# Tokens on partitions in the last MLP's output, an earlier context half in the convolution, another order in the opening

## The chip, the cores and the metric

The kernel runs on one core of one Trainium2 chip. The metric is device time of the whole kernel in microseconds (us); the kernel before takes 3229.1 us as the median of three runs (3225.97 to 3230.03). The trace is one further execution, recorded by the hardware profiler.

## The reference

Width 1024, 256 latent tokens (`x`) and 256 context tokens, all in fp32. Only the latents come out. Cut to the parts around the change:

```python
s_lat, s_ctx = silu(c), silu(c_ctx)
mod_l, mod_c = s_lat @ ada_w[i] + ada_b[i], s_ctx @ ada_w[i] + ada_b[i]     # six chunks of 1024 each
h_lat = rms_norm(x) * (1 + mod_l[1]) + mod_l[0]                             # opening: first layer's input
...                                                     # retention + FFN, differential attention + FFN
x = x + g * (silu(a) * b) @ ffn_w_out                                       # ffn1_out, latents only
# second model, layer 0: convolution mixer, on latents and context
u = x * (1 + sc1) + sh1                                                     # uc likewise, from ctx_2
a = u @ w_pw1 + b_pw1;  a = a[:, :1024] * sigmoid(a[:, 1024:])
a = dwconv(a, w_dw)                                                         # 31 taps per channel
...                                                     # pw2, layer norm, MLP, mLSTM layer
# second model, layer 1: the last MLP
h = layer_norm(ALPHA * h + g2 * (square(relu(modulate(h) @ w1)) @ w2), ln2_g, ln2_b)   # 1024 -> 4096 -> 1024
```

## The kernel before

One program with a hand-written stream for each engine and semaphores between them. The activations lie in `X[128, 8, 512]`: features on partitions in 8 chunks, tokens on the free dimension, latents in columns 0 to 255 (`L_COLS`), context in 256 to 511 (`C_COLS`).

**Matmuls.** Each fp32 product is three matmuls (`split_mm`, L622 to L626): both operands are split into a high and a low part, and high by high, low by high and high by low are added in one PSUM bank. The weights come as one list of 512 KB tiles of 128x1024, in the order of the table `PHASES`. A tile goes from SP's DMA into `RAW` (four slots) to ACT (`hi`, L1366 in the trace), to DVE (`lo`, L1848), to PE; the weights run three tiles ahead of PE (`LOOKAHEAD`). In nearly all phases the weights are the stationary operand and 256 or 512 tokens move. In `ml_o` it is the reverse: 128 tokens are stationary and 512 weight columns move. In `bank<-a,b` of the trace, a moves and b is stationary (`w_hi,xm_hi` is `ml_o`).

**Opening** (PE from L833, ACT, DVE from L2099). The 16 first tiles of the modulation weights (`ada_first`) are read by SP in order, then weight tiles 0 to 3. POOL's queue reads vectors, `X`, identity, ones and the rope table. PE waits for those, sums the squares of `X` (16 matmuls of 512 columns at L823), then multiplies tiles 11 to 15 (L841, 16 matmuls of two columns each). DVE forms the products of tiles 0 to 10 (L1859, twice per tile) with the reciprocal of the standard deviation (L1905) after tile 7, copies PE's part from PSUM (L2106), and builds the first `h_hi`, `h_lo`.

**ffn1_out and convolution.** `ffn1_out` is latents only. Then DVE adds the residual of 8 chunks (L1937, `residual`), and `modulate(4, TOK)` builds `h_hi`, `h_lo` chunk by chunk, latent half and context half (`h_lo` at L1924). PE waits for `x_upd` 32 (the latents' last residual) and has `h_lo_done` waits in its first tile. `pw1` has 16 weight tiles; a pair of tiles makes 128 channels of both halves of the gated unit. DVE's `conv_input(p)` (L2407 and on) turns the pair into `conv_in_hi`, `conv_in_lo` (L2420); PE's `conv_taps(p)` sums the taps with diagonal matrices. PE's order (from L1061):

```python
conv_taps(0)
for t in range(LOOKAHEAD, 16):
    pw1_tile(t)
    if t % 2 == 0:
        conv_taps(t // 2 - 1)
```

**Last MLP** (`mlp(1, ...)`, L1127). `mlp1_in` gives 4096 features, squared ReLU, kept as `mlp_hi`, `mlp_lo`; ahead of it PE sums features and squares for the layer normalisation and waits for `std_done`. `mlp1_out` is `gemm_cols`: 32 weight tiles, each stationary for 8 banks of 128 features x 256 tokens, 24 matmuls a tile. Then, one after the other: residual on DVE (L1937), `feature_sums` on PE (L829), mean and centering on DVE (L2067, L2069), squares on ACT and `square_sums` on PE (L823), the square root on ACT, `norm_x` on DVE (L1905, L2490, L2493), and one DMA of 1 MB (L511).

`own(...)` lets an engine wait for its own last instruction where the next one reads its result.

## Time and profile before

| What | Value |
|---|---|
| median of three runs | 3229.1 us (3225.97 to 3230.03) |
| the profiled execution's own time | 3219.72 us |
| its span, first instruction to last | 3217.8 us |
| mean granted TensorE clock | 0.974 of full speed |
| PE busy | 3056.8 us, 95% |
| DVE busy | 2058.1 us, 64% |
| ACT busy | 1200.0 us, 37% |
| POOL busy | 194.8 us, 6% |

The execution's own time is 1.92 us longer than its span. A matmul's length in the trace runs from issue to modelled end, and successive matmuls overlap, so the distance between starts is what a stream costs.

### The profile page before, as it was taken

Reading aid. Unit: us, or ns where it says so; the run is one execution under the profiler, and the core shown is the slowest. Engines: PE = TensorE matmul, PEld = TensorE weight load, DVE = VectorE, ACT = ScalarE, POOL = GpSimd, SP = SyncE. Lnnn points to the kernel's source line nnn. Section 1 sums busy time; section 2 is a strip of 40 time slices with the busy share of each in tenths; the row PEclk is TensorE's granted clock in tenths of the full one; section 3 lists DMA queues with packets and bytes.
Section 4 is the critical chain, followed back from the end, with each engine's and each line's share of the span. In section 5 each row is a group of like instructions: output and inputs, shape, how many; then the busy total and the mean of one; then the engine's idle time right before and its main releaser. Section 6 shows DMA issues by size and latency. Waiting matters only on the chain.

```text
span 3217.8 us, 43502 instructions
## 1 busy us (share of the span) xinstructions
PE 3056.8 (95%) x15904; PEld 2538.1 (79%) x15904; DVE 2058.1 (64%) x3192; ACT 1200.0 (37%) x1788; POOL 194.8 (6%) x165
## 2 busy tenths in 40 slices
PE   6999999999999899898999999999999999998998
PEld 4778578888887699776888887798778777966897
DVE  6963578877754756687798867542188433544654
ACT  3223434332243664554341324432245322312553
POOL 1300000000021000000030300000000000001110
PEclk8999999999999999999999999999999999988999
DMA  6662054666522156310266543662356332523453
GB/s 255 203 216 92 20 183 170 209 209 236 171 84 92 53 170 222 117 54 27 79 203 213 169 167 106 221 214 98 118 177 219 127 113 92 183 101 124 145 183 125
DMA packets 124806, 479.53 MB, mean 149 GB/s; under 512 B 13705, under 2 KB 14729, under 8 KB 122209
## 3 DMA queue, kind: packets, MB, share of 16 engines
q1 hardware_dynamic: 119984, 443.08, 40.6%
q0 software_dynamic: 4656, 34.17, 2.8%
q8 instruction: 114, 1.87, 0.2%
q14 instruction: 52, 0.42, 0.0%
HBM read 459.37 MB, written 17.83 MB: 148 GB/s over the span
## 4 chain that ended last, share of the span: by engine, by line
PE 83%; DVE 9%; ACT 3%; issue 3%; DMA 1%; SPq 0%; DVEq 0%; ACTq 0%; PEldq 0%
PE bank L624 25%; PE bank L625 24%; PE bank L626 24%; PE bank L1343 2%; PE bank L878 1%; PE bank L1292 1%; ACT tmp L1366 1%; DVE ada_junk_a L1859 1%; DVE w_lo L1848 1%; DVE diff_col L2333 1%; ACT w_hi L1366 1%; PE bank L1229 1%; DMA ada_first<-in_ada 0%; PE bank L823 0%; DVE ada_first L1859 0%
## 5 line engine op out<-in xcount | busy, mean ns | idle before, releaser
L1848 DVE TENSOR_TENSOR w_lo<-w_raw,w_hi 128x1024 fp32r<-128x1024 f32 x620 | 756.4, 1229 | 700.0 <-ACT w_hi L1366 682.7
L1366 ACT ACTIVATE w_hi<-w_raw 128x1024 fp32r<-128x1024 f32 x623 | 654.3, 1055 | 963.9 <-PE bank L626 936.8
L624 PE MATMUL bank<-h_hi,w_hi 128*128 128x512 f32 (+1 forms) x2160 | 748.2, 346 | 47.3 <-DVE h_lo L1924 21.9
L625 PE MATMUL bank<-h_lo,w_hi 128*128 128x512 f32 (+1 forms) x2160 | 738.8, 342 | 0.0
L626 PE MATMUL bank<-h_hi,w_lo 128*128 128x512 f32 (+1 forms) x2160 | 738.4, 342 | 0.0
L624 PEld LDWEIGHTS bank<-h_hi,w_hi 128*128 128x128 f32 x2160 | 414.7, 192 | 103.8 <-issue 47.2
L625 PEld LDWEIGHTS bank<-h_lo,w_hi 128*128 128x128 f32 x2160 | 415.0, 192 | 46.9 <-issue 1.2
L626 PEld LDWEIGHTS bank<-h_hi,w_lo 128*128 128x128 f32 x2160 | 414.6, 192 | 45.5
L624 PE MATMUL bank<-w_hi,xm_hi 128*128 128x512 f32 x512 | 199.5, 390 | 1.7 <-DVE tmp L2606 0.9
L626 PE MATMUL bank<-w_hi,xm_lo 128*128 128x512 f32 x512 | 199.3, 389 | 0.0
L625 PE MATMUL bank<-w_lo,xm_hi 128*128 128x512 f32 x512 | 199.2, 389 | 0.0
L624 PE MATMUL bank<-mlp_hi,w_hi 128*128 128x256 f32 (+1 forms) x528 | 175.8, 333 | 0.0
L625 PE MATMUL bank<-mlp_lo,w_hi 128*128 128x256 f32 (+1 forms) x528 | 174.8, 331 | 0.0
L626 PE MATMUL bank<-mlp_hi,w_lo 128*128 128x256 f32 (+1 forms) x528 | 174.8, 331 | 0.0
L624 PE MATMUL bank<-xm_hi,w_hi 128*128 128x512 f32 (+1 forms) x512 | 173.1, 338 | 1.7 <-issue 0.8
L626 PE MATMUL bank<-xm_hi,w_lo 128*128 128x512 f32 (+1 forms) x512 | 172.8, 337 | 0.0
L625 PE MATMUL bank<-xm_lo,w_hi 128*128 128x512 f32 (+1 forms) x512 | 172.7, 337 | 0.0
L1366 ACT ACTIVATE tmp<-bank 128x512 f32<-128x512 f32 (+1 forms) x124 | 62.3, 502 | 181.9 <-PE bank L626 107.4
L566 POOL TENSOR_TENSOR mlp_lo<-tmp,mlp_hi 128x512 f32 (+1 forms) x64 | 92.5, 1445 | 608.9 <-DVE tmp L2543 559.6
L624 PE MATMUL bank<-ffn_hi,w_hi 128*128 128x256 f32 (+1 forms) x360 | 120.3, 334 | 2.8 <-issue 1.4
L625 PE MATMUL bank<-ffn_lo,w_hi 128*128 128x256 f32 (+1 forms) x360 | 119.7, 332 | 0.0
L626 PE MATMUL bank<-ffn_hi,w_lo 128*128 128x256 f32 (+1 forms) x360 | 119.7, 332 | 0.0
(404 smaller groups left out, 4952.4 us busy)
## 6 DMA issues: line engine op xcount, KB each, us to landing
w_raw<-in_weights SPq DMA_DIRECT2D x623, 512.0 KB, 3.3
ada_ring_f<-in_ada SPq DMA_DIRECT2D x56, 512.0 KB, 3.2
ada_ring_g<-in_ada SPq DMA_DIRECT2D x44, 512.0 KB, 3.3
ada_ring_b<-in_ada SPq DMA_DIRECT2D x38, 512.0 KB, 4.2
ada_ring_a<-in_ada SPq DMA_DIRECT2D x32, 512.0 KB, 3.3
ada_first<-in_ada SPq DMA_DIRECT2D x16, 512.0 KB, 16.2
v_spill<-ml_v POOLq DMA_DIRECT2D x1, 4096.0 KB, 13.3
o_spill<-ml_o_grp POOLq DMA_DIRECT2D x4, 1024.0 KB, 4.8
```

The lines of the kernel that those rows point to most:

```text
L566: pool.tensor_tensor(mlo[:, t, 0:T], tmp(s % 2, T), mhi[:, t, 0:T].bitcast(F32), SUB)\
L624: mm(out, lhs[0], rhs[0], start=start, stop=False)
L625: mm(out, lhs[0], rhs[1], start=False, stop=False)
L626: return mm(out, lhs[1], rhs[0], start=False, stop=stop)
L878: last = mm(PS[3 + t][:, :], ATT[:, a, i0:i0 + P], RV[:, v, 512 * h:512 * (h + 1)], start=n == 0, stop=n == len(keys) - 1)
L1229: last = mm(PS[0][0:16, :], gate_part(2, f - 1), tmp((f - 1) % 2), start=f == 1, stop=f == MLC)
L1292: last = mm(PS[2 * (h % 2) + j // 2][:, (j % 2) * LAT:(j % 2 + 1) * LAT], MK[:, 4 * h + d, j * P:(j + 1) * P], MQ[:, 4 * h + d, :], start= ...
L1343: last = mm(PS[6 + n % 2][:, :], MPT(h, d)[:, j, t * P:(t + 1) * P], MV2[:, j, 512 * h:512 * (h + 1)], start=i == 0, stop=i == len(keys) - 1)
L1366: return nc.scalar.activation(out, in_, func, **kw)
L1848: V.tensor_tensor(WLO[:, slot, :], RAW[:, slot, :], WHI[:, slot, :].bitcast(F32), SUB)\
L1859: ins = V.scalar_tensor_tensor(junk[:, :] if st == 0 else tile, tile, 1.0, rows[:, st, :], MUL, MUL, accum_out=MOD[:, bass.ds(a * 2 + st, 1)])
L2333: own(V.reduce_max(DCOL[:, col + 12:col + 13], PS[2 * (u % 2) + m][:, :], AX.X))
```

## The change

**Opening.** SP reads `X` between modulation tiles 5 and 6 (before, POOL's queue did), and weight tiles 0 to 2 after modulation tile 9. A semaphore stands for two modulation tiles instead of four. PE takes tiles 3, 5, 7, 9, 11, 13 and 15, three of them ahead of the square sums and four behind; DVE takes the other nine, with the reciprocal after tile 12. The rope table is loaded after POOL's three `w_lo`.

**Convolution.** DVE and ACT build the context half of `pw1`'s input during `ffn1_out` (steps 8 to 16 of its 22). After `ffn1_out` only the latent half is left, and residual, product and low part of a chunk follow each other by chunk. PE waits for `x_upd` 28 instead of 32. `pw1_tile(3)` stands ahead of `conv_taps(0)`. One feature sum moves ahead of the last taps.

**Last MLP's output.** `out_tokens` makes 128 tokens stationary and moves 512 weight columns, the left column half first (16 weight tiles of two blocks of 128 rows x 512 columns), then the right one: 12 matmuls a tile, 384 in all. Between the halves PE turns `X` with 16 transposes. The last three tiles are used for tokens 0 to 127 first, then for tokens 128 to 255. The gate becomes a row: eight diagonal matrices built by DVE during `down`, two fp32 matmuls with ones ahead of `mlp1_in`, two copies on ACT. The layer normalisation is done on DVE per 128 tokens: gate product, sum, `bn_stats`, `bn_aggr`, centering, reciprocal and output, with the square root on ACT; the sums of the left half are done during the right one. Gain and bias come as rows by one DMA of 1 MB on POOL's queue. The output leaves in four DMAs of 256 KB. The three zero tiles at the end of the weight list are gone.

The diff, cut to its core:

```diff
+CTX2_AT = 8
...
+ADA_TENSOR = (3, 5, 7, 9, 11, 13, 15)
...
 for n in range(ADA_FIRST):
-    sp.dma_start(ADA_RAW[:, n, :], ada[n]).then_inc(S(f"ada_first{n // 4}"), 16)
-for n in range(SLOTS):
-    sp.dma_start(RAW[:, n, :], weights[n]).then_inc(raw_full[n], 16)
+    sp.dma_start(ADA_RAW[:, n, :], ada[n]).then_inc(S(f"ada_first{n // 2}"), 16)
+    if n == 5:
+        sp.dma_start(X[:, :, :], x_t).then_inc(S("x_first"), 16)
+    if n == 9:
+        for s in range(LOOKAHEAD):
+            sp.dma_start(RAW[:, s, :], weights[s]).then_inc(raw_full[s], 16)
+sp.dma_start(RAW[:, LOOKAHEAD, :], weights[LOOKAHEAD]).then_inc(raw_full[LOOKAHEAD], 16)
...
-sp.wait_ge(S("x_final"), DC)
-sp.dma_start(out_d, X[:, :, 0:LAT]).then_inc(S("stored"), 16)
-sp.wait_ge(S("stored"), 48)
+for t in range(2):
+    for half in range(2):
+        sp.wait_ge(S("tok_out"), N("tok_out", 2 * t + half + 1))
+        sp.dma_start(out_d[:, t, half, :], ZTOK[:, t, half, :]).then_inc(S("stored"), 16)
...
 pool.dma_start(VECS[:, :], vecs_d).then_inc(S("vecs_in"), 16)
-pool.dma_start(X[:, :, :], x_t).then_inc(S("x_in"), 16)
+pool.dma_start(ONES[:, :], consts_d[1]).then_inc(S("consts_in"), 16)
 pool.dma_start(IDENT[:, :], consts_d[0]).then_inc(S("consts_in"), 16)
-pool.dma_start(ONES[:, :], consts_d[1]).then_inc(S("consts_in"), 16)
-pool.dma_start(ROPE[:, :, :, :], ret_rope_d).then_inc(S("consts_in"), 16)
...
+pool.dma_start(ROPE[:, :, :, :], ret_rope_d).then_inc(S("vecs_in"), 16)
...
-pe.wait_ge(S("consts_in"), 48)
-square_sums(0, TOK, 0)
-
 pe.wait_ge(S("silu_c_done"), 1)
...
-for n in range(ADA_VECTOR, ADA_FIRST):
-    pe.wait_ge(S(f"ada_first{n // 4}"), 16 * 4)
-    col = 2 * (n - ADA_VECTOR)
+for i, n in enumerate(ADA_TENSOR):
+    if i == 3:
+        pe.wait_ge(S("consts_in"), 32)
+        square_sums(0, TOK, 0)
+    pe.wait_ge(S(f"ada_first{n // 2}"), 16 * 2)
     for k in range(DC):
-        last = mm(PS[7][:, col:col + 2], ADA_RAW[:, n, k * P:(k + 1) * P], vec("c_cols", 2 * k, 2),
+        last = mm(PS[7][:, 2 * i:2 * i + 2], ADA_RAW[:, n, k * P:(k + 1) * P], vec("c_cols", 2 * k, 2),
                   start=k == 0, stop=k == DC - 1)
 last.then_inc(S("ada_pe_done"), 1)
 pe.wait_ge(S("std_done"), 1)
...
-pe.wait_ge(S("x_upd"), 32)
+pe.wait_ge(S("x_upd"), 24 + 4)
...
-conv_taps(0)
 for t in range(LOOKAHEAD, 16):
     pw1_tile(t)
+    if t == LOOKAHEAD:
+        conv_taps(0)
     if t % 2 == 0:
         conv_taps(t // 2 - 1)
         if t >= 6:
             conv_feature_sum(t // 2 - 3)
+conv_feature_sum(DC - 3)
 conv_taps(DC - 1)
-for c in range(DC - 3, DC):
+for c in range(DC - 2, DC):
...
+def out_tokens(relu0, free0):
...
+    g0, n_half = FIRST["mlp1_out"], MLP_HALF_C
+
+    def block(half, s, t, start, stop):
+        slot = (g0 + n_half * half + s) % SLOTS
+        tok = slice(t * P, (t + 1) * P)
+        for kk in range(2):
+            k = 2 * s + kk
+            last = split_mm(PS[2 * t + half][:, :], (MHI1[:, k, tok], MLO1[:, k, tok]),
+                            w(slot, 512 * kk, 512), start and kk == 0, stop and kk == 1)
+        return last
+
+    for half in range(2):
+        tail = 0 if half == 0 else LOOKAHEAD
+        for s in range(n_half - tail):
+            pe.wait_ge(S("w_lo_done"), g0 + n_half * half + s + 1)
+            if half == 0:
+                pe.wait_ge(S("mlp_free"), free0 + 2 * s + 2)
+            for t in range(2):
+                if s == 0:
+                    pe.wait_ge(S("m_relu_done"), relu0 + 2 * t + half + 1)
+                last = block(half, s, t, s == 0, s == n_half - 1)
+                if s == n_half - 1 and t == 0:
+                    last.then_inc(S("y_tok"), 1)
+            last.then_inc(S("tile_done"), 1)
+        if half == 0:
+            pe.wait_ge(S("x_kept"), N("x_kept", 1))
+            pe.wait_ge(S("m_relu_done"), relu0 + 8)
+            for t in range(2):
+                for c in range(DC):
+                    last = nc.tensor.transpose(PS[4 + 2 * t + c // 4][:, c % 4 * P:(c % 4 + 1) * P],
+                                               X[:, c, t * P:(t + 1) * P], IDENT[:, :])
+            last.then_inc(S("x_turned"), 1)
+    for s in range(n_half - LOOKAHEAD, n_half):
+        pe.wait_ge(S("w_lo_done"), g0 + n_half + s + 1)
+        last = block(1, s, 0, False, s == n_half - 1)
+    last.then_inc(S("y_tok"), 1)
+    for s in range(n_half - LOOKAHEAD, n_half):
+        last = block(1, s, 1, False, s == n_half - 1)
+    last.then_inc(S("y_tok"), 1)
...
+        pe.wait_ge(S("g2_diag"), N("g2_diag", 1))
+        for half in range(2):
+            mm(PS[6 + half][:, :], ONES[:, :], G2DIAG[:, 4 * half:4 * half + 4, :]
+               .rearrange("p c n -> p (c n)"), start=True, stop=True).then_inc(S("g2_rows"), 1)
...
+        if j:
+            out_tokens(done + COUNT[ph_in] - 8, before + 8)
...
+    shift = shifts(2, 0)
+    for t in range(FFN_C):
+        hi_ahead("ffn1_out", t, t)
+        c = t - CTX2_AT
+        if 0 <= c < DC:
...
+            act.wait_ge(S("c4_raw"), N("c4_raw", c + 1))
+            f(HHI[:, c, C_COLS], hbuf(c)[:, C_COLS], ACT.Identity, bias=shift(c, 1)).then_inc(S("c4_hi"), 1)
...
+    f(CELL[:, 1:2], ONES[:, 0:1], ACT.Sqrt)
+    for t in range(2):
+        act.wait_ge(S("tok_var"), N("tok_var", t + 1))
+        f(ZCOL[:, t, 2:3], ZCOL[:, t, 1:2], ACT.Sqrt, bias=vec("eps", 1)).then_inc(S("tok_std"), 1)
...
-for n in range(ADA_VECTOR):
-    dve.wait_ge(S(f"ada_first{n // 4}"), 16 * 4)
+for n in range(ADA_FIRST):
+    if n in ADA_TENSOR:
+        continue
+    dve.wait_ge(S(f"ada_first{n // 2}"), 16 * 2)
     own(ada_product(n, ADA_RAW[:, n, :], AREA_A))
-    if n == 7:
+    if n == 12:
         inverse_std(0, TOK)
...
 dve.wait_ge(S("ada_pe_done"), 1)
-own(V.tensor_copy(MOD[:, 2 * ADA_VECTOR:2 * ADA_FIRST], PS[7][:, 0:2 * (ADA_FIRST - ADA_VECTOR)]))
+n_pe = len(ADA_TENSOR)
+first = 2 * ADA_TENSOR[0] - 2
+own(V.tensor_copy(MOD[:, first:first + 4 * n_pe].rearrange("p (a b) -> p a b", b=4)[:, :, 2:4],
+                  PS[7][:, 0:2 * n_pe].rearrange("p (a b) -> p a b", b=2)))
...
-        weights_only("ffn1_out", 6, 114, AREA_E)
...
+        for t in range(FFN_C):
+            lo_ahead("ffn1_out", t, t)
...
+            c = t - CTX2_AT
+            if 0 <= c < DC:
+                V.tensor_scalar(hbuf(c)[:, C_COLS], X[:, c, C_COLS], scale(c, 1), None, MUL)\
+                    .then_inc(S("c4_raw"), 1)
+            if 1 <= c <= DC:
+                dve.wait_ge(S("c4_hi"), N("c4_hi", c))
+                V.scalar_tensor_tensor(HLO[:, c - 1, C_COLS], hbuf(c - 1)[:, C_COLS], shift(c - 1, 1),
+                                       HHI[:, c - 1, C_COLS].bitcast(F32), ADD, SUB)
...
-    residual(f"ffn{layer}_out", T, layer, 5, x0)
+
+        def lat_low(c):
+            dve.wait_ge(S("h_hi_done"), 4 * DC + c + 1)
+            V.scalar_tensor_tensor(HLO[:, c, L_COLS], hbuf(c)[:, L_COLS], shift(c, 0),
+                                   HHI[:, c, L_COLS].bitcast(F32), ADD, SUB).then_inc(S("h_lo_done"), 1)
+        for c in range(DC):
+            bank_ready(dve, "ffn1_out", c)
+            V.scalar_tensor_tensor(X[:, c, L_COLS], PS[c][:, L_COLS], mod(1, 5, c, 0), X[:, c, L_COLS], MUL, ADD)\
+                .then_inc(S("x_upd"), 1)
+            if c:
+                lat_low(c - 1)
+            if c >= 4:
+                dve.wait_ge(S("h_lo_done"), 4 * DC + c - 3)
+            dve.wait_ge(S("x_upd"), x0 + c + 1)
+            V.tensor_scalar(hbuf(c)[:, L_COLS], X[:, c, L_COLS], scale(c, 0), None, MUL).then_inc(S("raw_done"), 1)
+        lat_low(DC - 1)
...
-dve.wait_ge(S("x_in"), 32)
-modulate(4, TOK, *mods(2, 0), normed=False)
...
+def tok_sum(t, half):
+    z = ZTOK[:, t, half, :]
+    own(V.tensor_tensor(z, PS[2 * t + half][:, :], G2ROW[:, half, :], MUL))
+    own(V.tensor_tensor(z, z, PS[4 + 2 * t + half][:, :], ADD))
...
+def tok_stats(t, half):
+    own(V.bn_stats(ZSTAT[:, t, 6 * half:6 * half + 6], ZTOK[:, t, half, :]))
...
+def tok_var(t):
+    V.bn_aggr(ZCOL[:, t, 0:2], ZSTAT[:, t, :]).then_inc(S("tok_var"), 1)
...
+def tok_centered(t, half):
+    z = ZTOK[:, t, half, :]
+    V.scalar_tensor_tensor(z, z, ZCOL[:, t, 0:1], LNROWS[:, 0, 512 * half:512 * half + 512], SUB, MUL)
...
+def tok_out(t, half):
+    z = ZTOK[:, t, half, :]
+    V.scalar_tensor_tensor(z, z, ZCOL[:, t, 3:4], LNROWS[:, 1, 512 * half:512 * half + 512], MUL, ADD)\
+        .then_inc(S("tok_out"), 1)
...
+def tok_rstd(t):
+    dve.wait_ge(S("tok_std"), N("tok_std", t + 1))
+    own(V.reciprocal(ZCOL[:, t, 3:4], ZCOL[:, t, 2:3]))
...
+def tok_norm():
+
+    for t in range(2):
+        dve.wait_ge(S("y_tok"), N("y_tok", t + 2))
+        tok_sum(t, 1)
+        tok_stats(t, 1)
+        tok_var(t)
+        dve.wait_ge(S("tok_var"), N("tok_var", t + 1))
+        for half in range(2):
+            tok_centered(t, half)
+        tok_rstd(t)
+        for half in range(2):
+            tok_out(t, half)
...
-            weights_and_keep(ph_out, T)
-        if j or n == 0:
+            for t in range(COUNT[ph_out] - LOOKAHEAD):
+                lo_ahead(ph_out, t, t)
+                if 4 <= t < 4 + DC:
+                    keep_x(t - 4, T)
+                if t == 4 + DC:
+                    dve.sem_inc(S("x_kept"), 1)
+
+                if t in (18, 21):
+                    if t == 18:
+                        dve.wait_ge(S("tile_done"), FIRST[ph_out] + MLP_HALF_C)
+                        dve.wait_ge(S("x_turned"), N("x_turned", 1))
+                        dve.wait_ge(S("g2_copied"), N("g2_copied", 2))
+                    tok_sum(t // 3 - 6, 0)
+                if t in (19, 22):
+                    tok_stats(t // 3 - 6, 0)
+            dve.wait_ge(S("ln_rows_in"), N("ln_rows_in", 16))
...
-weights_only("down")
+for t in range(COUNT["down"]):
+    lo_ahead("down", t, t)
+    if t == 4:
+        for c in range(DC):
+            last = V.tensor_scalar(G2DIAG[:, c, :], IDENT[:, :], mod(3, 5, c, 0), None, MUL)
+        last.then_inc(S("g2_diag"), 1)
...
+return w.reshape(-1, 2, P, 2, 512).transpose(3, 0, 2, 1, 4).reshape(-1, P, 1024)
```

PE's order in the opening. Rows name out, operands (`ada_first` is a tile of the modulation weights, `tmp` the squares of `X`), the shape moved and how many follow each other. Before:

```order
L618 UNCONDITIONAL_BRANCH
L823 MATMUL bank<-tmp,ones 128x512 x8
L841 MATMUL bank<-vecs,ada_first 128x2 x40
L624 MATMUL bank<-h_hi,w_hi 128x512
L625 MATMUL bank<-h_lo,w_hi 128x512
```

And of the changed kernel:

```order
L655 UNCONDITIONAL_BRANCH
L879 MATMUL bank<-vecs,ada_first 128x2 x24
L862 MATMUL bank<-tmp,ones 128x512 x8
L879 MATMUL bank<-vecs,ada_first 128x2 x32
L661 MATMUL bank<-h_hi,w_hi 128x512
L662 MATMUL bank<-h_lo,w_hi 128x512
```

Three tiles (24 matmuls) now stand ahead of the squares' sums, and four (32) behind them. (In the trace a matmul of fp32 operands has two rows, here one.)

PE's order where the first taps begin (`h_hi`, `w_hi` are `pw1`'s input and weights, `conv_in` the taps' input, `conv_diag` the diagonal matrices; bank 3 holds `pw1`'s tile 2, bank 4 its tile 3). Before:

```order
L624 MATMUL bank3<-h_hi_53,w_hi_50 128x512
L625 MATMUL bank3<-h_lo_54,w_hi_50 128x512
L626 MATMUL bank3<-h_hi_53,w_lo_51 128x512
L624 MATMUL bank2<-conv_in_hi_112,conv_diag_hi_118 128x512
L625 MATMUL bank2<-conv_in_lo_113,conv_diag_hi_118 128x512
```

And of the changed kernel:

```order
L661 MATMUL bank4<-h_hi_53,w_hi_50 128x512
L662 MATMUL bank4<-h_lo_54,w_hi_50 128x512
L663 MATMUL bank4<-h_hi_53,w_lo_51 128x512
L661 MATMUL bank2<-conv_in_hi_112,conv_diag_hi_118 128x512
L662 MATMUL bank2<-conv_in_lo_113,conv_diag_hi_118 128x512
```

The taps followed directly on tile 2; now the 24 matmuls of tile 3 stand between.

DVE's order at the end, from the last low parts of the weights on (`z_tok` is the output with tokens on partitions, `z_stat` and `z_col` its statistics, `ln_rows` gain and bias). Before:

```order
L1848 TENSOR_TENSOR w_lo<-w_raw,w_hi 128x1024 x20
L1937 SCALAR_TENSOR_TENSOR x_res<-bank,mod,x_res 128x256 x8
L2067 TENSOR_SCALAR tmp<-bank 128x256
L2069 TENSOR_TENSOR x_res<-x_res,tmp 128x256 x8
L1905 RECIPROCAL tmp<-tmp 128x256
L2490 TENSOR_TENSOR x_res<-x_res,tmp 128x256 x8
L2493 TENSOR_SCALAR x_res<-x_res,vecs 128x256 x8
```

And of the changed kernel, for the first 128 tokens and the start of the second:

```order
L1959 TENSOR_TENSOR w_lo<-w_raw,w_hi 128x1024 x6
L2630 TENSOR_TENSOR z_tok<-bank,g_row 128x512
L2631 TENSOR_TENSOR z_tok<-z_tok,bank 128x512
L2634 BN_STATS z_stat<-z_tok 128x6
L2637 BN_AGGR z_col<-z_stat 128x2
L2641 SCALAR_TENSOR_TENSOR z_tok<-z_tok,z_col,ln_rows 128x512 x2
L2650 RECIPROCAL z_col<-z_col 128x1
L2645 SCALAR_TENSOR_TENSOR z_tok<-z_tok,z_col,ln_rows 128x512 x2
L2630 TENSOR_TENSOR z_tok<-bank,g_row 128x512
```

Of the 34 operations behind the last `w_lo`, 18 of 512 columns or fewer are left, and no matmul stands between them.

## Rows read from the trace of the kernel before

**Rows 1.** The page: the chain that ended last, by engine.

```profile
PE 83%; DVE 9%; ACT 3%; issue 3%; DMA 1%; SPq 0%; DVEq 0%; ACTq 0%; PEldq 0%
```

**Rows 2.** Windows: PE, PEld, DVE, ACT, POOL busy (instructions); clock; DMA share; GB/s.

```profile
3105.00:3194.50 89.50, 89.50 (x747) 89.40 (x745) 45.18 (x50) 32.83 (x31) 0.00 (x0) 1.00 0.50 167
3194.50:3217.80 23.30, 8.27 (x33) 5.37 (x32) 13.11 (x33) 3.82 (x10) 0.00 (x0) 0.77 0.13 45
```

**Rows 3.** PE's timeline (start, length): first and last of `mlp1_out`'s 768 matmuls.

```profile
3102.28 0.28 PE L624 MATMUL bank<-mlp_hi,w_hi 128*128 128x256 f32 x1
...
3194.32 0.28 PE L626 MATMUL bank<-mlp_hi,w_lo 128*128 128x256 f32 x1
```

**Rows 4.** PE's timeline in `ml_o`: a matmul and the thirtieth after it.

```profile
2378.83 0.39 PE L624 MATMUL bank<-w_hi,xm_hi 128*128 128x512 f32 x1
...
2385.63 0.39 PE L624 MATMUL bank<-w_hi,xm_hi 128*128 128x512 f32 x1
```

**Rows 5.** PE's timeline at the mLSTM's transposes.

```profile
2320.38 0.65 PE L1224 MATMUL bank<-ident,ml_v 128*128 128x128 f32 x4
2320.96 1.03 PE L1229 MATMUL bank<-tmp,x_res 128*16 128x512 f32 x2
```

**Rows 6.** Timeline of the tail: SP's queue issues the output.

```profile
3212.58 0.66 SPq L511 DMA_DIRECT2D out_t<-x_res  x1
```

**Rows 7.** By tile: nanoseconds min/median/max. Page: DMA issues, KB, us to landing.

```profile
L2765 DVE TENSOR_TENSOR ml_h<-ml_h,ml_o x8: 681/688/692, 2862.1 to 2925.3; 128x512 f32<-128x512 f32 x8
L2769 DVE BATCH_NORM_STATS2 tmp<-ml_h x8: 674/680/684, 2863.3 to 2926.5; 128x6 f32<-128x512 f32 x8
...
L2346 DVE SCALAR_TENSOR_TENSOR diff_p<-diff_e,diff_col x16: 750/752/754, 1038.5 to 1081.8; 128x512 f32<-128x512 f32 x16
...
w_raw<-in_weights SPq DMA_DIRECT2D x623, 512.0 KB, 3.3
...
out_t<-x_res SPq DMA_DIRECT2D x1, 1024.0 KB, 4.8
```

**Rows 8.** PE's timeline: first of `pw1`, of the taps, of `pw1`'s fourth tile ([idle before <-releaser]).

```profile
1325.94 0.77 PE L624 MATMUL bank<-h_hi,w_hi 128*128 128x512 f32 x1 [5.95 <-DVE h_lo L1924]
...
1349.09 0.76 PE L624 MATMUL bank<-conv_in_hi,conv_diag_hi 128*128 128x512 f32 x1 [4.81 <-DVE conv_in_lo L2420]
...
1359.74 0.39 PE L624 MATMUL bank<-h_hi,w_hi 128*128 128x512 f32 x1
```

**Rows 9.** DVE's timeline: residuals, and the first instruction of `conv_input` 0, 1 and 3.

```profile
1320.06 3.23 DVE L1937 SCALAR_TENSOR_TENSOR x_res<-bank,mod,x_res 128x256 f32<-128x256 f32 x8
...
1345.95 0.75 DVE L2407 SCALAR_TENSOR_TENSOR conv_in<-bank,vecs,tmp 128x512 f32<-128x512 f32 x1
...
1365.39 0.75 DVE L2407 SCALAR_TENSOR_TENSOR conv_in<-bank,vecs,tmp 128x512 f32<-128x512 f32 x1 [1.40 <-PE bank L626]
...
1405.28 0.75 DVE L2407 SCALAR_TENSOR_TENSOR conv_in<-bank,vecs,tmp 128x512 f32<-128x512 f32 x1 [2.31 <-PE bank L626]
```

**Rows 10.** PE's timeline in the opening, and a window of it (columns of Rows 2).

```profile
18.24 9.43 PE L823 MATMUL bank<-tmp,ones 128*128 128x512 f32 x16 [18.24 <-DMA ret_rope<-in_ret_rope]
29.12 1.92 PE L841 MATMUL bank<-vecs,ada_first 128*128 128x2 f32 x16 [1.45 <-DMA ada_first<-in_ada]
34.15 13.81 PE L841 MATMUL bank<-vecs,ada_first 128*128 128x2 f32 x64 [3.11 <-DMA ada_first<-in_ada]
55.72 0.77 PE L624 MATMUL bank<-h_hi,w_hi 128*128 128x512 f32 x1 [7.76 <-DVE h_lo L1924]
...
34.10:48.00 13.90, 13.81 (x64) 13.73 (x64) 13.76 (x14) 3.17 (x3) 8.24 (x3) 0.50 0.83 322
```

**Rows 11.** DVE's timeline in the opening.

```profile
18.85 1.23 DVE L1859 SCALAR_TENSOR_TENSOR ada_junk_a<-ada_first,c_rows 128x1024 f32<-128x1024 f32 x1 [18.85 <-DMA ada_first<-in_ada]
...
40.31 3.35 DVE L1905 RECIPROCAL tmp<-tmp 128x512 f32<-128x512 f32 x1
...
51.88 0.17 DVE L2106 COPY mod<-bank 128x10 f32<-128x10 f32 x1
```

134 lines of the change are left out of this document (85 added, 49 removed).

## The prediction

> **What bounds the kernel now.** I read the chain of work that ended last first: 83% of it is PE, 9% DVE, 3% ACT [rows 1]. So time is won in two ways only: a stream that costs PE less, or a place where PE waits. The change touches three places, and each gets its own view.
>
> The last MLP's output is the first kind. In its window PE is busy for all 89.50 us at full clock while DVE is busy half of it [rows 2]. The second row there is the tail behind it: 23.30 us in which no engine works more than 13.1. That is a chain handed from engine to engine, the second kind.
>
> The convolution and the opening are of the second kind too. PE's timeline has a wait of 5.95 us ahead of `pw1`, one of 4.81 ahead of the first taps [rows 8], and one of 7.76 before the first weight matmul at 55.72, after four modulation tiles at half clock (0.50 in the window) [rows 10].
>
> **Last MLP, the stream.** 768 matmuls of 256 columns start from 3102.28 to 3194.32 [rows 3]: 92.04/767 = 0.120 us each, 92.2 in all. For 512 moving weight columns against stationary tokens I take `ml_o`, the same form: 6.80 us for 30 starts, 0.2267 each [rows 4]. 384 of them are 87.05 us, so 5.1 less. The same columns are moved (196,608 both times), so all of this is the cost per instruction. The lengths in the rows (0.28, 0.39) are not spacings.
>
> Here a rule can be weighed. The rows make 256 columns cost 120 ns and 512 cost 227 ns. The Trainium skill, page "TensorE: Matmul & The Clock Gate", section "Back-to-back issue gap", gives an isolated gap of columns over 2.4 plus 2.5 ns: 109 and 216 ns. By it the streams would cost 83.9 and 82.9 us, a gain of 1.0 instead of 5.1, and it speaks against this part. Neither of its figures is in the rows, and the narrow one is further off.
>
> Added are 16 transposes of 128x128. Four listed at 2320.38 are followed by the next matmul at 2320.96 [rows 5]: 0.145 each, 2.3 in all. (Ends: nothing, if they overlap better; 4, if the switch costs as much again.) The stream's end comes 5.1 - 2.3 = **2.8 us earlier**, the last matmul starting at 3191.5 on the old scale. Feeding keeps up: a weight tile then takes PE 12 x 0.2267 = 2.72 us instead of 24 x 0.120 = 2.88, and DVE is busy 45.18 of 89.50 [rows 2].
>
> **Last MLP, the tail.** Before, 23.5 us pass from the last start to the span's end (3217.8 - 3194.32 [rows 3]), the output's DMA issued at 3212.58 [rows 6]. After, the last three weight tiles do tokens 0 to 127 first, so these are complete 18 x 0.2267 = 4.08 us before the rest. DVE's work on 128 tokens, at [rows 7]: two sums at 0.69 (one reads PSUM, so up to 0.75), `bn_stats` 0.68, an aggregate and a reciprocal on one or two columns with the hand-over at about 0.2 each, two centerings and two outputs at 0.75 less the overlap that back-to-back instructions show: 1.4 + 0.7 + 0.4 + 1.4 + 1.4 = 5.4 us with a little for `own`. It has four such hand-overs; bounds 5.0 and 6.5. ACT's square root hides behind the two centerings. Measured from the last matmul's start: tokens 0 to 127 ready at -4.08 + 0.5; 5.4 later 1.8; the second 5.4 ends at 7.2. Then the last DMA of 256 KB. Landing took 3.3 us for 512 KB and 4.8 for 1024 [rows 7]: the slope is 1.5 per 512 KB, so 2.55, and I take 2.7. The other three DMAs are issued 0.7 us or more before and overlap. With 0.4 to the end: 10.3 us instead of 23.5, **13.2 less**. Bounds 10.5 (both tokens' blocks 1.1 longer, a queued DMA 0.5) and 14.2.
>
> The Trainium skill, page "DMA: Bandwidth & Descriptors", section "Anatomy of one DMA — SWDGE (gpsimd) path", gives a fixed 2.0 us and bytes over 436 GB/s; for 256 KB that would be an estimate of 2.6 us. The rows' own line through two sizes gives the same for this queue, so splitting the output costs no fixed part on the path.
>
> Side work costs nothing here: the gate's two matmuls fall into PE's wait for the standard deviation ahead of `mlp1_in`; eight products for the diagonals (0.3 us each) lie in `down`, where DVE waits for PE; the 1 MB of gain and bias has the whole of `mlp1_in` to land. If the two ACT copies were late, `mlp1_in`'s tiles 6 and 7 would wait, 1 us at most.
>
> **Convolution.** Before, PE restarts at 1325.94, when residuals (3.23 us for eight [rows 9]) and the first chunk are done. After, DVE does residual 0.42, product 0.25 and low part 0.45 per chunk, latents only, about 1.33 with its waits for ACT; PE needs four residuals: restart at about 1324.1, 1.8 earlier. The first taps need `conv_input(0)`, which began at 1345.95 [rows 9] and came to PE at 1349.09 [rows 8]. It now begins 2.0 earlier (the first matmuls at half clock, too) and ends at 1347.1. PE is in tile 3 then, 24 x 0.2267 = 5.4 us, until 1347.5: the 4.81 us wait is covered and so are the 2.1 us that the clock costs behind it (the first taps' row is 0.76 instead of 0.39).
>
> But the stall moves. DVE's round from one `conv_input` to the next is 1365.39 - 1.40 - 1345.95 = 18.04 us of work [rows 9]. The second cannot begin before 1344.0 + 18.0 = 1362.0, and reaches PE 3.1 later, at 1365.1. PE, with taps 0 (8.5 at full clock) and tile 4 (5.6) behind it, is there at 1361.7: a new wait of 3.4 us ahead of the second taps. The waits of 5.95 and 4.81 were followed by half clock [rows 8]; if this one is too, another 2.1. Carried to `conv_input(3)`, from where PE sets the pace (DVE there waits 2.31 for it [rows 9]): 1405.28 becomes 1399.7 without the fall, 1401.8 with it. I take the fall, **3.5 less**. Bounds: 1.5 (PE waits in `ffn1_out` too, where ACT and DVE now hand a chunk to and fro for about 3.1 us a tile against PE's 2.9, some 2 us over eight tiles against a lead of three tiles) and 7.
>
> **Opening.** PE starts at 18.24, held by POOL's loads, and the modulation tiles are then bound by their DMA: tile 11 was in at 29.12, tile 15 at 34.15, so 1.26 us per 512 KB [rows 10]. Tile 15 had 23 such units up to it (rows 1 MB, `X` 2 MB, rope 0.5 MB, 16 tiles), 29.0 us, so the stream begins at 5.1. In the new order tile 7 is unit 14, in at 22.8; tile 13 unit 23, at 34.1; tile 15 unit 25, at 36.7. One tile takes PE 1.92 us at full clock, and four took 13.81 at half, about 3.44 each [rows 10]. PE does 3 and 5 early, 7 from 22.8 to 26.2 (half clock, after waiting), the sums (9.43) to 35.7, then four tiles, two at either clock, 10.7, to 46.4. DVE takes 2.41 us a tile: tile 12 by 36.5, reciprocal (3.35 [rows 11]) by 40.2, tile 14 by 42.6, and some 2 lost beside POOL's `w_lo` (three of them, 8.24 us in that window): 44.5. So PE is last, by 2. From the copy of PE's part to the first weight matmul are 55.72 - 51.88 = 3.84 [rows 10, 11]; 46.4 + 3.84 = 50.2, **5.5 less**. Bounds: all seven slow (2.4 less), all fast, DVE last (7.4 less).
>
> **The sum.** 2.8 + 13.2 + 3.5 + 5.5 = 25.0, from 3219.72 to 3194.7 for an execution like the profiled one. That one was 9.4 us below the median of the runs (3229.1), which is what the next median stands beside: 3229.1 - 25.0 = **3204**. All bounds together on one side: 2.8 + 10.5 + 1.5 + 2.4 less 1.7 (transposes), 15.5; on the other 5.1 + 14.2 + 7 + 7.4, 33.7; they are independent, so 18 to 32: **3197 to 3211**.
>
> **Rivals.** *The forecast as summed*, 0.66.
>
> *The opening gives nothing*: PE has seven tiles instead of five, and at 3.44 each the three ahead of the sums delay these as well. With the sums starting 1 to 2 late and four slow tiles behind (13.8), PE is done at 50.5 to 51.5 and the weight matmuls begin at 54.3 to 55.3: the sum falls to 20 or 21, 3208 to 3209. For it speaks 0.50 in the window; against, the 1.92 of the first tile after the sums. 0.13.
>
> *More than summed*: no half clock behind the new 3.4 us wait (2.1), and PE's tiles fast in the opening (1.9) with a shorter DVE chain (1): 3197 to 3199. 0.11.
>
> *Columns alone count*: the wide stream saves only what the gap rule gives, 1 instead of 5.1, and the transposes eat it. 3208. Against it speaks the spacing seen in both forms [rows 3, 4]. 0.05.
>
> *Too little to tell*: the parts cancel, within 0.2% (6.5 us, about what a measurement of this kernel tells from no change); 0.02.
>
> *Slower*: the form of the last stream differs from `ml_o`, and the 0.39 us listed for one wide matmul is its real spacing there, because stationary tokens are reloaded for every 512 columns from tiles in another layout. 384 x 0.39 = 149.8 instead of 92.2, 57.6 more, and 2.3 for the transposes, against 22.2 of other gains: 37.7 slower, 3267. It decides from a spacing of 0.29 on (384 x 0.29 = 111.4: 19.2 and 2.3 eat the 22.2). Against it: the same reload at 0.2267 [rows 4]. With anything unseen, 0.03.
>
> Faster by over 0.2%: 0.66 + 0.13 + 0.11 + 0.05 = 0.95; same 0.02; slower 0.03.
>
> **What would show it.** In the new trace: starts 0.227 apart in `mlp1_out`, and its last one about 10.3 before the span's end; no reciprocal of 256 columns and no matmul after it. No wait ahead of the first taps, one of 3 to 4 ahead of the second, and the row behind it at 0.39 or 0.76. The first weight matmul at 50. It is wrong if a wait appears in `mlp1_out` for `w_lo` (the split halves free slots otherwise), if PE waits for context chunks in `ffn1_out`, or if the squares in the opening are held by `X`, now behind six tiles on one queue.

## The result, and the profile after

| | median, us | runs |
|---|---|---|
| before, the runs of this measurement | 3227.53 (3225.05 to 3230.03) | 4 |
| changed | 3194.02 (3192.34 to 3195.41) | 4 |
| ratio changed to before | 0.9899, 95% interval 0.9884 to 0.9915 | |
| before, all timed executions, with those that the experiments brought | 3224.35 (3218.0 to 3234.1) | 85 |
| changed, likewise | 3194.1 (3191.7 to 3202.1) | 14 |

The kernel is faster by 33.5 us in the first measurement and by 30 over all executions. The prediction said 25 and a time of 3204, with a range of 3197 to 3211. The time lies below it. The profiled executions tell another story: their spans are 3217.8 and 3193.8, 24.0 apart. Both must be explained.

The page of the changed kernel: head and chain.

```profile
span 3193.8 us, 42620 instructions
...
PE 83%; DVE 9%; ACT 3%; issue 3%; DMA 1%; SPq 1%; DVEq 0%; ACTq 0%; PEldq 0%
```

PE is busy for 3052.8 us where it was busy for 3056.8: 4.0 of the 24.0 us, so most of the gain is idle time. The opening, from PE's timeline (start, length, idle before and what ended it), against [rows 10]:

```profile
12.86 6.96 PE L879 MATMUL bank<-vecs,ada_first 128*128 128x2 f32 x32 [12.86 <-DMA ada_first<-in_ada]
22.79 3.58 PE L879 MATMUL bank<-vecs,ada_first 128*128 128x2 f32 x16 [2.97 <-DMA ada_first<-in_ada]
26.23 9.03 PE L862 MATMUL bank<-tmp,ones 128*128 128x512 f32 x16
35.10 9.57 PE L879 MATMUL bank<-vecs,ada_first 128*128 128x2 f32 x64
49.90 0.76 PE L661 MATMUL bank<-h_hi,w_hi 128*128 128x512 f32 x1 [5.23 <-DVE h_lo L2035]
```

and VectorE's there, against [rows 11]:

```profile
36.78 3.35 DVE L2016 RECIPROCAL tmp<-tmp 128x512 f32<-128x512 f32 x1
40.17 2.68 DVE L1970 SCALAR_TENSOR_TENSOR ada_junk_a<-ada_first,c_rows 128x1024 f32<-128x1024 f32 x1
42.78 3.35 DVE L1970 SCALAR_TENSOR_TENSOR ada_first<-ada_first,c_rows 128x1024 f32<-128x1024 f32 x1
46.18 0.17 DVE L2221 COPY mod<-bank 128x14 f32<-128x14 f32 x1
```

Tile 7 came at 22.79, as counted. PE finished at 44.7, VectorE at 46.1: the last tile's two products took 2.68 and 3.35 us instead of 1.22, beside GpSimd's `w_lo`. VectorE is last, not PE as the prediction had it, but the first weight matmul starts 5.8 us earlier (said: 5.5).

The convolution, PE's timeline with the two gaps that are left, against [rows 8]:

```profile
1321.04 0.80 PE L661 MATMUL bank<-h_hi,w_hi 128*128 128x512 f32 x1 [5.29 <-DVE x_res L2401]
...
1345.46 0.40 PE L661 MATMUL bank<-conv_in_hi,conv_diag_hi 128*128 128x512 f32 x1
...
1362.79 0.48 PE L661 MATMUL bank<-conv_in_hi,conv_diag_hi 128*128 128x512 f32 x1 [3.10 <-DVE conv_in_lo L2562]
1363.11 0.40 PE L662 MATMUL bank<-conv_in_lo,conv_diag_hi 128*128 128x512 f32 x1
...
1364.16 0.63 PE L663 MATMUL bank<-conv_in_hi,conv_diag_lo 128*128 128x512 f32 x1
1364.59 0.63 PE L661 MATMUL bank<-conv_in_hi,conv_diag_hi 128*128 128x512 f32 x1
...
1483.70 0.47 PE L661 MATMUL bank<-conv_in_hi,conv_diag_hi 128*128 128x512 f32 x1 [2.29 <-issue]
```

The wait ahead of the first taps is gone, and one of 3.10 us stands ahead of the second (said: 3.4). The matmul behind it has 0.48 and the next 0.40, as at full clock. But the half clock only comes later: from 1364.16 on, 1.4 us behind the wait, seven matmuls have 0.63 and start 0.43 apart instead of 0.24. The twentieth matmul of these taps starts 6.12 us after the first, and 4.61 behind a wait that full clock follows (the one of 2.29): the fall came, and cost 1.5 us (said: 2.1). So the first matmul behind a wait does not tell.

VectorE's `conv_input` 0 and 3, against [rows 9]:

```profile
1341.68 0.75 DVE L2549 SCALAR_TENSOR_TENSOR conv_in<-bank,vecs,tmp 128x512 f32<-128x512 f32 x1
...
1399.01 0.75 DVE L2549 SCALAR_TENSOR_TENSOR conv_in<-bank,vecs,tmp 128x512 f32<-128x512 f32 x1 [2.30 <-PE bank L663]
```

Counted from the start of the last matmul of `ffn1_out` (1319.71 before, 1315.47 here), `pw1` starts at 5.57 instead of 6.23, but `conv_input(0)` at 26.21 instead of 26.24: nothing of the earlier restart arrives, since behind it eleven matmuls of 0.63 follow instead of seven. `conv_input(3)` starts at 83.54 instead of 85.57, 2.0 earlier (said: 3.5).

The last MLP's output and tail, against [rows 3] and [rows 6]:

```profile
3095.52 0.40 PE L661 MATMUL bank<-w_hi,mlp_hi 128*128 128x512 f32 x1
...
3139.07 1.91 PE L1203 MATMUL bank<-ident,x_res 128*128 128x128 f32 x16
3140.74 0.48 PE L661 MATMUL bank<-w_hi,mlp_hi 128*128 128x512 f32 x1
...
3184.14 0.39 PE L663 MATMUL bank<-w_hi,mlp_lo 128*128 128x512 f32 x1
```

```profile
3185.84 0.68 DVE L2630 TENSOR_TENSOR z_tok<-bank,g_row 128x512 f32<-128x512 f32 x1
...
3189.77 1.42 DVE L2645 SCALAR_TENSOR_TENSOR z_tok<-z_tok,z_col,ln_rows 128x512 f32<-128x512 f32 x2
```

The second block of tokens on VectorE is the timeline's part above (its first and its last row); the stores stand among the DMA issues:

```profile
out_t<-z_tok SPq DMA_DIRECT2D x4, 256.0 KB, 2.0
```

192 wide matmuls take 3139.07 - 3095.52 = 43.55 us, 0.2268 each; the transposes 1.67. From the first start to the last it is 88.62 us instead of 92.04. From the last start to the span's end it is 9.66 instead of 23.5. A block of tokens costs VectorE 5.3 us (said: 5.4), and a 256 KB DMA lands in 2.0 by the median of the four (said: 2.7).

### The profile page after: what moved, and what is told of

Read it like the earlier page. It is cut to its first block, busy times and chain, and to the rows that moved or that the text cites. A ratio compares the mean times of both kernels' runs of the same rounds, so it can differ in the third digit from the quotient of the medians.

```text
span 3193.8 us, 42620 instructions
## 1 busy us (share of the span) xinstructions
PE 3052.8 (96%) x15540; PEld 2521.4 (79%) x15540; DVE 2053.7 (64%) x3179; ACT 1194.3 (37%) x1780; POOL 193.4 (6%) x165
## 4 chain that ended last, share of the span: by engine, by line
PE 83%; DVE 9%; ACT 3%; issue 3%; DMA 1%; SPq 1%; DVEq 0%; ACTq 0%; PEldq 0%
PE bank L661 25%; PE bank L662 24%; PE bank L663 24%; PE bank L1434 2%; PE bank L916 1%; PE bank L1383 1%; DVE ada_junk_a L1970 1%; DVE w_lo L1959 1%; ACT tmp L1457 1%; DVE diff_col L2477 1%; ACT w_hi L1457 1%; PE bank L1320 1%; DMA ada_first<-in_ada 0%; DVE x_res L2061 0%; PE bank L1351 0%
## 5 line engine op out<-in xcount | busy, mean ns | idle before, releaser
L661 PEld LDWEIGHTS bank<-w_hi,xm_hi 128*128 128x128 f32 x512 | 96.1, 188 | 23.3 <-issue 3.0
L663 PEld LDWEIGHTS bank<-w_hi,xm_lo 128*128 128x128 f32 x512 | 96.1, 188 | 20.2
L662 PEld LDWEIGHTS bank<-w_lo,xm_hi 128*128 128x128 f32 x512 | 96.1, 188 | 19.7
```

The source lines that it names most:

```text
L661: mm(out, lhs[0], rhs[0], start=start, stop=False)
L662: mm(out, lhs[0], rhs[1], start=False, stop=False)
L663: return mm(out, lhs[1], rhs[0], start=False, stop=stop)
```

## Experiments

**The control and the three parts alone.** `before_again` is the kernel before, with no edit. The parts, in short:

```diff
# a_only: the opening
-ADA_VECTOR = 11
+ADA_TENSOR = (3, 5, 7, 9, 11, 13, 15)
...
+                if n == 5:
+                    sp.dma_start(X[:, :, :], x_t).then_inc(S("x_first"), 16)
...
# b_only: the convolution
-            pe.wait_ge(S("x_upd"), 32)
+            pe.wait_ge(S("x_upd"), 24 + 4)
...
+                if t == LOOKAHEAD:
+                    conv_taps(0)
...
# c_only: the last MLP's output
-                        gemm_cols(ph_out, T, mhi, mlo, "mlp_free", before + 8, relu_left)
+                        out_tokens(done + COUNT[ph_in] - 8, before + 8)
```

> The kernel before, unchanged, as a control. Theory 1 (the profiled execution of before, 3219.7, was a lucky one, and its timed runs differ from it by some place that the trace can show): this trace has a span near 3224 to 3227, and beside the first trace some single waits or clock falls are longer, 5 to 8 us in all. Theory 2 (the chips differ, and the first trace came from another one): all executions here agree within 3 us, and the extra time is spread over the whole span, or sits in the DMA-bound stretches. In both the ratio to before is 1.000 within 0.001.

> Only the opening is changed. By the sum of the prediction 5.5 us less than before (first weight matmul at 50 instead of 55.7); if the missing 8 us of the median sit in the opening of before (its loads on two queues landing later in other executions) 10 to 14 us less, and the first weight matmul of the control well behind 55.7.

> Only the convolution is changed (the context half in ffn1_out, tile 3 ahead of the first taps, residual and latent half by chunk). By the sum 3.5 us less; if the half clock behind the new wait does not come 5.6. If the missing time sits here, 8 to 12 less.

> Only the last MLP's output is changed. By the sum 16 us less (stream 2.8, tail 13.2); the trace of the change shows 17.1. If the missing time sits here, 22 to 25 less: the old tail would then be longer in other executions than the 23.5 us of the first trace.

Medians: control 3223.5 (11 executions), before beside them 3223.8 (24); opening alone 3214.2, ratio 0.9971 (0.9959 to 0.9982); convolution alone 3219.3, 0.9985 (0.9976 to 0.9993); last MLP alone 3203.9, 0.9938 (0.9925 to 0.9951). So 9.6, 4.6 and 19.9 us, 34 in all, each 1 to 4 more than its term. The control's eleven executions, on one chip, spread from 3219.5 to 3228.0, and the medians of before on the five chips used lie between 3222.0 and 3225.4, so the spread is not one between chips. The stages in the traces are steadier. Each figure is a difference of two starts on PE's timeline (the last one: first start of `mlp1_out` to the span's end):

| us | before | control | a_only | b_only | c_only | changed |
|---|---|---|---|---|---|---|
| first weight matmul | 55.72 | 55.88 | 49.60 | 55.66 | 55.61 | 49.90 |
| end of `ffn1_out` to `pw2` | 203.46 | 203.82 | 203.98 | 200.49 | 203.28 | 200.83 |
| `mlp1_out` to the end | 115.52 | 115.54 | 115.51 | 115.54 | 98.12 | 98.28 |

Every part works in its own stage, and none shows in another's: 5.8 to 6.1 us, 2.6 to 3.0 and 17.2 to 17.4 against the first trace of before. The first phase behind the opening gives about another 0.5 (its end is at 144.85 in before and at 144.5 to 145.7 in four more traces with the old opening, and at 138.2 to 140.4 in eleven with the new one and no filling).

The control shows where the rest comes from. Its span is 3226.0, 8.2 longer than the first trace of the same kernel, and most of that (6.3 us, by the starts of the same matmuls at 889 and 988 us of the first trace) arises there, in the differential attention. Windows of the first trace of before (columns as in rows 2):

```profile
885.00:890.00 5.00, 3.05 (x22) 2.60 (x21) 4.78 (x11) 2.65 (x6) 0.00 (x0) 1.00 0.22 76
890.00:895.00 5.00, 5.00 (x43) 4.94 (x42) 4.82 (x10) 2.46 (x6) 0.00 (x0) 1.00 0.00 0
```

and of the control:

```profile
885.00:890.00 5.00, 3.05 (x17) 2.44 (x17) 4.30 (x8) 2.65 (x9) 0.97 (x2) 1.00 0.44 156
890.00:895.00 5.00, 5.00 (x28) 4.71 (x27) 4.82 (x13) 3.58 (x9) 0.00 (x0) 0.66 0.01 3
```

In both, PE has just waited 1.95 us for the same `h_lo`. In one execution full clock follows (43 matmuls in 5 us), in the other 0.66 (28 matmuls; the half clock comes 1.4 us behind the wait). More such places follow, and executions differ in them.

**More executions, a shifted opening, the order alone, later taps.** `after_again` is the changed kernel. The others:

```diff
# a_late: a_only, and
+            for _ in range(5):
+                own(V.tensor_tensor(AREA_A[0][:, :], AREA_A[0][:, :], AREA_A[0][:, :], ADD))
             modulate(0, TOK, *mods(0, 0))
# b_order: before, and
-            conv_taps(0)
             for t in range(LOOKAHEAD, 16):
                 pw1_tile(t)
+                if t == LOOKAHEAD:
+                    conv_taps(0)
# taps_later: changed, and
-                if t == LOOKAHEAD:
-                    conv_taps(0)
-                if t % 2 == 0:
-                    conv_taps(t // 2 - 1)
...
+                if t % 2 == 1:
+                    conv_taps((t - 3) // 2)
...
```

> The changed kernel, unchanged, for more executions and a second trace. Theory 1 (before has a spread of 10 us between its executions, from half-clock stretches around 890 to 1000 us that some executions have and others not, and the first four timed ones of before lay high in it): here the median stays at 3193 to 3197, before at 3223 to 3224 on the same chip, so the change is worth 27 to 30 us and not 33.5. Theory 2 (the changed kernel is really 33 us faster): the ratio stays at 0.990.

> The kernel with only the opening changed, and five idle additions of 1024 columns (6.1 us) on VectorE before the first modulation, so that the first weight matmul is back at 55.7. a_only was 9.6 us below before by its median, though its first weight matmul is only 5.8 to 6.2 earlier. If where in time the differential attention falls decides on its half-clock stretches, this kernel is at 3223 to 3224, as before. If the rest of the gain comes with the opening's own content, it stays 3 us below before, 3220.

> Only one line of the convolution's change: tile 3 of pw1 ahead of the first taps, in the kernel before. By the prediction's steps the wait of 4.8 us goes, and one of about 3.4 appears ahead of the second taps, since VectorE's round of 18 us sets the second one: 3.5 us less if no half clock follows the new wait, 1.4 less if it does. The other parts (context half early, residual by chunk) would then be worth 1 to 3.

> The changed kernel with all taps one tile later (taps p behind tile 2p+3, so the second ones behind tile 5). If the wait of 3.1 us ahead of the second taps is a wait for VectorE that PE can fill with tile 5 (5.4 us), it goes, and the kernel is 2.5 to 3.5 us faster than the changed one: 3191. The rival: VectorE's round of 18 us is the bound, and the wait only moves to the third taps (1 to 2 us there), so 1 to 2 are left.

`after_again`: 3194.9 against 3225.4 (23 executions of before), 0.9908 (0.9894 to 0.9922). `a_late`: first weight matmul at 56.19, 3222.3, 0.9991 (0.9983 to 1.0000): 3.1 faster, though its opening is no shorter than before's. Neither expectation fits clearly (3223 to 3224, or 3220), the interval holds both. No place in its trace shows a gain (its span is 3218.2, that of before 3217.8), so this difference is probably one between executions; it is not shown.

`b_order`: 3222.6, 0.9992 (0.9982 to 1.0003). The trace says why one line is not enough. Its wait moved as expected, and it reaches the wait ahead of the last taps 1.9 us sooner (168.38 instead of 170.25 behind `ffn1_out`). Then:

```profile
1489.35 0.76 PE L624 MATMUL bank<-conv_in_hi,conv_diag_hi 128*128 128x512 f32 x1 [3.14 <-issue]
```

Twelve matmuls at half clock follow that wait (before it seven), so 19.2 us pass to the square sums instead of 18.0, and the stretch from these to `pw2` has a granted clock of 0.82 instead of 0.92 and takes 16.7 us instead of 15.2. `pw2` begins 204.29 behind `ffn1_out`, 0.8 later than before. What was won is given back by the clock, twice. Against the changed kernel, which reaches the last taps at 168.23, the 168.38 here say that the order of tile 3 and the first taps gains this part of the stage, and the context half and the earlier restart 0.15 us.

`taps_later` shows the same with more at stake: no wait ahead of the second taps, the last taps start 2.9 sooner (165.32 instead of 168.23), although the wait ahead of them is 4.37 instead of 2.29, and there

```profile
1478.90 0.76 PE L661 MATMUL bank<-conv_in_hi,conv_diag_hi 128*128 128x512 f32 x1 [4.37 <-issue]
```

half clock follows for twelve matmuls, where the changed kernel's trace has none: 18.51 us instead of 15.92 to the square sums. `pw2` comes at 200.51, the changed kernel's is at 200.83. The median is 3193.7. So of the wait that was filled and the half clock that went with it, 2.1 us came back as a longer wait for VectorE (in both kernels the last taps start 3.1 us after its last `conv_input`), and 2.6 of the 2.9 that were left went to the clock behind it.

**The parts of the tail and of the opening, and the moved sum.** Edits of the changed kernel:

```diff
# one_store
-            for t in range(2):
-                for half in range(2):
...
-                    sp.dma_start(out_d[:, t, half, :], ZTOK[:, t, half, :]).then_inc(S("stored"), 16)
+            sp.dma_start(out_d, ZTOK[:, :, :, :]).then_inc(S("stored"), 16)
...
# no_split: the last three weight tiles
-                    last = block(1, s, 0, False, s == n_half - 1)
...
+                    for t in range(2):
+                        last = block(1, s, t, False, s == n_half - 1)
...
# five_tiles
-ADA_TENSOR = (3, 5, 7, 9, 11, 13, 15)
+ADA_TENSOR = (7, 9, 11, 13, 15)
# sum_back
-            conv_feature_sum(DC - 3)
             conv_taps(DC - 1)
-            for c in range(DC - 2, DC):
+            for c in range(DC - 3, DC):
```

> The changed kernel with one output DMA of 1 MB after the last normalised half, instead of four of 256 KB. By the prediction's slope the last landing goes from 2.6 to 4.8 us: the time from the last matmul's start to the end of the span goes from 9.66 to 11.9, 2.2 more. Rival: four small DMAs queue behind each other and gain nothing, then it stays at 9.7.

> The changed kernel with the last three weight tiles used for both blocks of tokens in turn, so that tokens 0 to 127 are complete 6 matmuls (1.36 us) before the rest and not 18 (4.08). If VectorE's chain of two blocks is what follows the last matmul, the time from its start to the end of the span is 2.7 longer, 12.4. Rival: PE's reordering is worth nothing, because VectorE's first block waits for something else.

> The changed kernel with modulation tiles 7, 9, 11, 13 and 15 on PE and 3 and 5 back on VectorE (one tile ahead of the square sums, four behind), the loads in the new order. If the order of the loads is what gained, VectorE fits two tiles (4.8 us) into its waits of 2.6 and 4.0 us, and the first weight matmul stays at 49.9 to 50.5. If PE's two more tiles gained, it comes 4.8 later, at 54.7.

> The changed kernel with the sixth feature sum back behind the last taps. From the wait ahead of the last taps to the start of the square sums the changed kernel takes 15.92 us, kernels without this edit 17.9 to 19.2. If the edit does it, here 18 to 19.2, of which 0.9 is the sum itself, which no longer fills the wait, and the rest the clock, which falls when PE waits 3.1 instead of 2.3 us there. If it is another part of the change, it stays at 15.9 plus 0.9.

`one_store` (3195.0): last start 3180.32, end 3191.6, so 11.3 instead of 9.66 (expected: 11.9). The 1 MB DMA landed in 3.9 us and not 4.8, so four stores are worth 1.6. `no_split` (3197.6): 3185.11 to 3197.5, 12.4: 2.7 longer, to the tenth. VectorE's two blocks are the chain behind the last matmul.

`five_tiles` (3199.1):

```profile
26.06 9.38 PE L862 MATMUL bank<-tmp,ones 128*128 128x512 f32 x16
35.27 9.03 PE L879 MATMUL bank<-vecs,ada_first 128*128 128x2 f32 x64
50.21 0.77 PE L661 MATMUL bank<-h_hi,w_hi 128*128 128x512 f32 x1 [5.91 <-DVE h_lo L2035]
```

The first weight matmul stays at 50.2, so PE's two extra tiles gained nothing: VectorE did them while it waited for loads. The time was gained by the rest of the change: the order of the loads, a semaphore for two tiles, tiles that alternate between PE and VectorE, and one of PE's ahead of the square sums; no run parts these. The median is 5 us longer than the changed kernel's, and all four executions lie at 3197.8 to 3199.7. The trace has that time in code that the edit does not touch: it is 0.3 us behind the changed kernel's at the first weight matmul, and 5.1 behind at the end of the differential attention. Why all four executions lie high is not shown.

`sum_back` (3196.8): the wait is 3.14, its matmul 0.77, and 17.84 us pass to the square sums. But these then run at 0.91 instead of 0.83 and take 15.2 instead of 16.7, and `pw2` comes at 201.07 instead of 200.83. Moving the sum gave 1.9 us in its stage and 0.2 in all. It does it by the wait: of the eleven traces whose wait there is 2.29, nine have full clock behind it and two (`after_more`, `no_split`) half clock, with 17.3 us to the square sums; all eight traces whose wait there is 3.14 or more have half clock behind it.

**Filled waits.** Matmuls of ones by ones into an unused bank while PE waits, in the opening (`fill_open`), or there, ahead of `pw1` and ahead of `pw2` (`fill_all`); `after_more` is the changed kernel.

```diff
+            for _ in range(18):
+                mm(PS[6][:, 0:P], ONES[:, :], ONES[:, :], start=True, stop=True)
             pe.wait_ge(S("std_done"), 1)
```

> The changed kernel once more, for the spread between executions. By the stages that the change touches (opening 6.0, convolution 2.8, last MLP 17.4) it is worth 26.2 us, which is also the difference of the fastest executions so far (3218.0 and 3191.9). If the 3 to 4 us by which the medians differ more are the draw, this median lies at 3195 to 3198; if they are real, at 3194 to 3195 again and before at 3223 to 3225.

> The changed kernel with 18 matmuls of ones by ones (128 columns, into an unused bank) on PE behind the last modulation tile, where PE otherwise waits 5.2 us for the first h_lo. If the half clock behind a wait comes from PE's idleness, the first weight matmuls are 0.227 us apart instead of 0.43, and 1.6 us are won by the end of the first tile. If the clock there has another cause (power, loads), nothing changes but the wait's length.

> The same filling in three waits: the opening (18), ahead of pw1 (16, after the first residual) and ahead of pw2 (26, behind the square sums). Each stage behind them shows its first matmul at 0.39 instead of 0.77 and takes 1.6 to 2.1 us less: 3189 to 3191. If a filled wait only moves the fall to a later, shorter wait (as happened behind the moved feature sum), the stage gains and the total does not.

`after_more`: 3193.2 against 3222.7, 0.9917 (0.9903 to 0.9930). It did not go up to 3195 to 3198. In its trace the wait ahead of the last taps shows the draw inside the changed kernel, by a wait of the same length as above:

```profile
1479.91 0.76 PE L661 MATMUL bank<-conv_in_hi,conv_diag_hi 128*128 128x512 f32 x1 [2.29 <-issue]
```

`fill_open`:

```profile
44.15 6.92 PE L883 MATMUL bank<-ones 128*128 128x128 f32 x36
50.82 0.48 PE L661 MATMUL bank<-h_hi,w_hi 128*128 128x512 f32 x1
51.14 0.40 PE L662 MATMUL bank<-h_lo,w_hi 128*128 128x512 f32 x1
```

The weight matmuls start at full clock, and the first phase takes 87.18 us instead of 88.68. So PE's idleness brings the half clock. The filling ran 0.9 too long and took most of it back (3195.3). In `fill_all` (3192.4) the filling of the opening ended even later, and the first weight matmul comes at 53.52, 3.6 late; `ffn1_out` to `pw2` fell to 197.31, 3.5 less. The full clock behind `pw2`'s own wait gained nothing more: its second wait, for `w_lo`, grew from 2.00 to 4.21, and its first tiles take 20.8 us at either clock, since VectorE ends them.

**GpSimd's memset.** In the changed kernel PE restarts ahead of `pw1` 0.66 us sooner, not 1.84. The timeline of that place, without ACT's rows:

```profile
1315.82 0.48 DVE L2401 SCALAR_TENSOR_TENSOR x_res<-bank,mod,x_res 128x256 f32<-128x256 f32 x1
1315.82 1.97 POOL L592 MEMSET conv_in<- 128x2256 f32 x1 [326.07 <-PE bank L663]
1316.34 1.60 DVE L2408 TENSOR_SCALAR tmp<-x_res,mod 128x256 f32<-128x256 f32 x1
...
1318.91 0.35 DVE L2408 TENSOR_SCALAR tmp<-x_res,mod 128x256 f32<-128x256 f32 x1
```

The first product takes 1.60 us, the others 0.35, and it ends 0.15 us behind the memset.

```diff
# memset_late
-            pool.wait_ge(S("tile_done"), FIRST["ffn1_out"] + COUNT["ffn1_out"])
+            pool.wait_ge(S("h_lo_done"), 5 * DC)
             own(pool.memset(CIN[:, :, :], 0.0))
# memset_fill: that, and ahead of the wait for x_upd 28
+            pe.wait_ge(S("x_upd"), 24 + 1)
+            for _ in range(10):
+                mm(PS[0][:, 0:P], ONES[:, :], ONES[:, :], start=True, stop=True)
```

> The changed kernel with GpSimd's memset of the convolution's input moved from the end of ffn1_out to behind the last h_lo. In the trace of the changed kernel the first of eight VectorE products of 128x256 there takes 1600 ns and the other seven 347, and it ends 0.15 us after GpSimd's memset (1.97 us, started 0.5 before it). If GpSimd holds it up, all eight take 350 here and PE waits 4.05 instead of 5.29 us ahead of pw1. If the first product of its kind is slow for its own sake (its code), nothing changes.

> The same with 10 matmuls of ones on PE in what is left of that wait. The wait becomes 2 us or less, the first matmul of pw1 takes 0.40 to 0.50 instead of 0.80, and from the end of ffn1_out to the wait ahead of the last taps the kernel takes 1.2 plus 1.7 us less than the changed one (168.2, so 165.3). The rival, as in taps_later and b_order: VectorE's round of 18 us makes the wait ahead of the second taps longer by what is won, and 1 or less is left at the end.

All eight products of `memset_late`, by line (nanoseconds min/median/max), and PE's restart:

```profile
L2408 DVE TENSOR_SCALAR tmp<-x_res,mod x8: 347/348/353, 1315.4 to 1324.7; 128x256 f32<-128x256 f32 x8
```

```profile
1318.85 0.80 PE L661 MATMUL bank<-h_hi,w_hi 128*128 128x512 f32 x1 [4.04 <-DVE x_res L2401]
```

`ffn1_out` to `pw2` is 198.57 us, 2.3 less than in the changed kernel: the 1.25 of the wait, and 1.0 because five matmuls of 0.63 follow it instead of eleven. With the filling none does (the first takes 0.50, the next 0.39), and the last taps start at 165.16, as expected (165.3). But `conv_input(0)` starts only 0.8 sooner than in `memset_late`, the wait ahead of the second taps grows to 3.69, and `pw2` is at 197.94, 0.6 sooner. Medians 3192.0 and 3190.3 (four executions each), the lowest of all kernels here, though only the stage shows the gain beyond doubt.

## Why the prediction was wrong

**The sum of 25 held against the profiled execution, in part by luck.** It gave 3219.72 - 25.0 = 3194.7. The profiled execution of the changed kernel took 3195.4, and the median of 14 is 3194.1. The stages that the change touches give 26.2 there; stages that it does not touch were 2.1 longer in this trace than in that of before. The mechanisms of the last MLP held. In the opening VectorE was last and not PE, and in the convolution the earlier restart came to nothing.

**The step that failed** is "which is what the next median stands beside: 3229.1 - 25.0". Three executions were taken for the kernel's level, and the fourth, 9.4 us lower, for an exception. The 85 timed executions of before lie between 3218 and 3234, with the median at 3224.35: the three lay 4.8 us high, the profiled one 4.6 low. Nor had the range, made of the bounds of the terms alone, anything for this: from 3224.35 the same 18 to 32 would have been 3192 to 3206, with the result inside. Of the 10.0 us between 3204 and 3194.0, 4.8 are this base.

**Terms that were mis-sized.** Tail: 13.8, not 13.2 (mainly the DMA, which lands in 2.0, not 2.7). Stream: 3.4, not 2.8 (transposes 0.104 each, not 0.145). Opening: 5.8, and 0.5 in the phase behind it, not 5.5. Convolution: 2.6, not 3.5, and by other steps than the sum's. Its step "It now begins 2.0 earlier", for `conv_input(0)`, failed: the restart came 0.66 earlier and not 1.84 (GpSimd's memset, shown by `memset_late`, which has the other 1.25), the half clock behind it lasted longer, and 0.03 us arrived. Half clock behind the new wait came, as charged, and cost 1.5 instead of 2.1. The moved feature sum, which the sum did not price, gave 2.1 from the start of the last taps to the square sums, and the clock behind these took 1.5 back. By the steps, roughly: 3.5 - 2.0 + 0.5 + 0.6 = 2.6. All terms together are 26.2 instead of 25.0, so 1.2 of the 10.0.

**What stays open.** 30.3 us between the medians less 26.2 by the stages leaves 4.1. The fastest executions of either kernel (3218.0, 3191.7) differ by 26.3, as the stages do, but the median of before lies 6.3 above its fastest and that of the changed kernel 2.4. In the two traces of before, the slower one loses its time to half-clock stretches at waits that the change does not touch. From the first weight matmul to the last of `ffn1_out`, the stretch with these waits, five traces with the old opening take 1263.0 to 1271.9 us (median 1265.3), and thirteen with the new one 1262.0 to 1270.2 (median 1265.4; two of the five and none of the thirteen are above 1271). So the traces show no gain there by their medians, and with such a spread they are too few to exclude one. Whether the rest is chance over 14 executions or an effect of the changed opening (`a_only` and `a_late` have 3 us more than their stages too, and `five_tiles` lies 5 higher) the runs do not decide.

**The rivals.** Equal cost per column is out: 0.2268 in the new stream. The Trainium skill, page "TensorE: Matmul & The Clock Gate", section "Back-to-back issue gap", gives an isolated gap of 0.216 us for the wide and 0.109 for the narrow form; the traces show 0.227 and 0.120, and the measurement decides. The opening that gives nothing is out, as is the slow wide form. "More than summed" is nearest in time, but its reasons are not those found: the clock did fall at the new wait, and VectorE's chain in the opening was longer and not shorter; only PE's tiles there were faster than counted (done at 44.7, said 46.4). Of the output, one DMA of 1 MB lands in 3.9 (in the new layout) and 256 KB in 2.0, where the line through the two sizes of before had 2.55. The estimate of 2.6 us for 256 KB, worked out from the figures of the Trainium skill, page "DMA: Bandwidth & Descriptors", section "Anatomy of one DMA — SWDGE (gpsimd) path", is 0.6 too long for this queue; the measurement decides.

## What to carry to other kernels

Take the level of a kernel from many executions, and compare an edit by the length of its own stage in two traces: here the stages agreed within 0.6 us in most traces where whole executions differed by 10. Do not judge the clock behind a wait by its first matmul; the fall can come more than 1 us later. A wait that is filled can come back in part at the next hand-over to the engine that sets the round, and a longer wait may bring half clock with it; follow the stage to its end before counting the gain. Look at what the third engine does beside the one on the path.

## What the hardware showed unexpectedly

**One wait, two clocks.** The same 1.95 us wait in the same kernel was followed by full clock in one execution and by a stretch at 0.66 in another. Behind the wait of 2.29 ahead of the last taps, nine traces have full clock (the twentieth matmul starts 4.61 us after the first) and two have a first matmul of 0.76 with six at half clock behind it (6.0). Behind the waits of 3.10 to 5.19 us ahead of taps the clock fell in all traces, for at least five and at most twelve matmuls behind the first: at once (`c_only`, first matmul 0.76), or after one at full clock (`before_again`, 0.47), or after four (`after`, 0.48). With PE kept busy through 5 us, full clock followed.

**A memset that stops VectorE.** A memset of 1.97 us on GpSimd held a product of 128x256 with one tensor source in SBUF for 1.60 instead of 0.35 us, while the residual beside it, whose first source is in PSUM, took its usual 0.48. With the memset moved away, all eight products took 0.35. The Trainium skill, page "SBUF — State Buffer", section "SBUF: two separate sides", says that VectorE and GpSimd share a pair of ports under an exclusive lock, held for the whole instruction, so that a VectorE operation in a two-port mode waits for a running GpSimd instruction, and one with two SBUF sources waits for a GpSimd instruction that reads SBUF. The traces agree, though they do not show in which mode the product runs: it ended 0.15 us behind the memset's end, and in the opening operations with two SBUF sources took 2.68 and 3.35 us instead of 1.22 beside GpSimd's `w_lo`, which reads SBUF; no run took that `w_lo` away.
